# Stick-breaking attention inside a three-layer stack: running products of sigmoids in place of logarithms and suffix sums

## The reference, cut to what matters

```python
logits = einsum("bhtd,bhsd->bhts", q[:, :, s0:end], kb) * (Dh ** -0.5)
mask = s_idx[None, :] < t_idx[:, None]            # key strictly before query
log_keep = where(mask, log_sigmoid(-logits), 0.0)
after = sum(log_keep, -1, keepdims=True) - cumsum(log_keep, -1)
wts = where(mask, exp(log_sigmoid(logits) + after), 0.0)
outs.append(einsum("bhts,bhsd->bhtd", wts, vb))   # queries in blocks of 128
o = concatenate(outs) * silu(z)                   # z: a gate, 1024 channels
return o @ w_out
```

## Time and profile before

| | |
|---|---|
| median of three runs | 1218.24 us |
| the profiled execution: span from first to last instruction | 1214.8 us |
| what the runs' time has beside this span | 3.4 us |
| PE busy over the span | 96% |
| DVE, ACT, POOL busy over the span | 40%, 44%, 31% |
| stick-breaking stage, from the first piece of `last_gate` to the first `dense_unit` behind it | 628.1 to 753.4 us |

### The profile page before, as it was taken

How to read it: one execution, slowest core, us unless ns; L and a number is a source line. 1 busy time by engine, 2 the same in 40 slices (tenths; PEclk the granted TensorE clock), 3 DMA queues, 4 the chain that set the end, 5 groups by cost and what they waited for, 6 DMA issues and landing times.

```text
span 1214.8 us, 21306 instructions
## 1 busy us (share of the span) xinstructions
PE 1169.5 (96%) x8938; PEld 916.0 (75%) x8938; DVE 481.9 (40%) x903; ACT 539.0 (44%) x924; POOL 370.9 (31%) x148
## 2 busy tenths in 40 slices
PE   5999999989989999999999999999999999999898
PEld 3788886667668888777776667887887777678777
DVE  4575544553324382350314553640202333231563
ACT  4232246734336344542557774333135443753530
POOL 0133442233165414343431001323143231443161
PEclk7999999999999999999999999999999999999999
DMA  9723321386630232323423100333033411223301
GB/s 319 237 70 104 102 76 65 104 272 226 200 110 2 70 105 70 104 70 104 106 65 103 26 15 1 118 98 104 25 98 103 113 51 64 96 78 137 110 1 70
DMA packets 105761, 121.15 MB, mean 100 GB/s; under 512 B 5144, under 2 KB 91704, under 8 KB 105672
## 3 DMA queue, kind: packets, MB, share of 16 engines
q1 hardware_dynamic: 101424, 116.14, 30.2%
q10 hardware_dynamic: 4248, 3.73, 1.0%
HBM read 111.47 MB, written 2.10 MB: 93 GB/s over the span
## 4 chain that ended last, share of the span: by engine, by line
PE 84%; ACT 6%; DVE 4%; issue 3%; DMA 1%; ACTq 0%; SPq 0%; POOL 0%; DVEq 0%
PE ps L2043 41%; PE ps L2849 4%; PE ps L2663 3%; PE ps L2654 2%; PE ps L2089 2%; PE ps L2431 2%; PE ps L2184 2%; PE ps L2667 2%; PE ps L2693 2%; PE ps L2127 1%; PE ps L2207 1%; PE ps L2815 1%; PE ps L2260 1%; PE ps L2458 1%; PE ps L2802 1%
## 5 line engine op out<-in xcount | busy, mean ns | idle before, releaser
L606 POOL TENSOR_TENSOR wlo<-raw,whi 128x2048 fp32r<-128x2048 f32 x53 | 245.1, 4625 | 577.6 <-ACT whi L770 565.1
L770 ACT ACTIVATE whi<-raw 128x2048 fp32r<-128x2048 f32 x52 | 99.3, 1911 | 203.5 <-PE ps L2043 162.9
L612 POOL TENSOR_TENSOR wlo<-raw,whi 128x2048 fp32r<-128x2048 f32 x10 | 46.4, 4640 | 111.5 <-ACT whi L859 63.3
L1279 ACT ACTIVATE p<-sc,nmx 128x256 f32<-128x256 f32 x64 | 32.0, 501 | 47.0 <-PE ps L2802 45.8
L1870 DVE CUSTOM_DVE_ANT_0 sc<-ps,biast 128x256 f32<-128x256 f32 (+1 forms) x64 | 22.5, 393 | 66.8 <-PE ps L2791 37.9
L859 ACT ACTIVATE whi<-raw 128x2048 fp32r<-128x2048 f32 x11 | 21.1, 1917 | 62.8 <-PE ps L2043 62.8
L2043 PE MATMUL ps<-hC_hi,whi 128*128 128x512 f32 x184 | 47.1, 398 | 0.8 <-POOL wlo L606 0.8
L2043 PE MATMUL ps<-hC_lo,whi 128*128 128x512 f32 x184 | 45.6, 390 | 0.0
L2043 PE MATMUL ps<-hC_hi,wlo 128*128 128x512 f32 x184 | 45.4, 389 | 0.0
L2043 PEld LDWEIGHTS ps<-hC_hi,whi 128*128 128x128 f32 x184 | 33.8, 188 | 14.8 <-issue 6.4
L2043 PEld LDWEIGHTS ps<-hC_lo,whi 128*128 128x128 f32 x184 | 34.6, 188 | 7.4
(11 more groups left out here) (518 smaller groups left out, 2853.0 us busy)
## 6 DMA issues: line engine op xcount, KB each, us to landing
raw<-in_w_in_dram SPq DMA_DIRECT2D x24, 1024.0 KB, 5.2
raw<-in_w_in_a_dram SPq DMA_DIRECT2D x16, 1024.0 KB, 5.7
raw<-in_w_ada_dram SPq DMA_DIRECT2D x8, 1024.0 KB, 5.2
late_w<-in_w_ada_dram SPq DMA_DIRECT2D x8, 1024.0 KB, 6.1
raw<-in_w_kv_dram SPq DMA_DIRECT2D x8, 1024.0 KB, 5.1
raw<-in_w_in_b_dram SPq DMA_DIRECT2D x8, 1024.0 KB, 5.3
ada_a<-in_w_ada_dram SPq DMA_DIRECT2D x4, 1024.0 KB, 10.1
ada_b<-in_w_ada_dram SPq DMA_DIRECT2D x4, 1024.0 KB, 13.2
```

Source lines behind the costliest of these rows:

```text
L606: pool.tensor_tensor(wlo[:, s, :], raw[:, s, :], whi[:, s, :].bitcast(F32), ALU.subtract).then_inc(lo_ready, 1)
L612: pool.tensor_tensor(wlo[:, s, :], raw[:, s, :], whi[:, s, :].bitcast(F32), ALU.subtract).then_inc(lo_ready, 1)
L770: A(whi[:, s, :], raw[:, s, :], ACT.Copy).then_inc(hi_ready, 1)
L1279: A(p2[:, n % 2, 256 * e:256 * e + 256], sc2[:, n % 2, 256 * e:256 * e + 256], ACT.Exp, scale=-1.0, bias=nmx[:, grp, t, 2 * hp + e:2 * hp ...
```

## The change: what it does

Keys now lie along columns and queries along partitions; the product along the keys is a scan along a row. Two heads (one group kt) are worked together, in three rounds: the fourth block of queries (2 x 512 columns), the third (2 x 384), and the second with the first (2 x (256 + 128)). There are 24 rounds.

For round r: TensorE makes the scores of both heads at once, one on each half of the rows (`scores`); ACT makes sigmoid(-logit) (`keeps`) and sigmoid(logit) (`takes`) from PSUM; DVE turns the keeps into running products from the last key to the first, in place, by one scan instruction with a second operand `restart` that is 1 where the next head begins (`scans`, the third round has two scans); POOL multiplies takes by the products shifted by one key (`weights`); TensorE turns the weights by transposes (`turns`, three rounds later); ACT evacuates one head's half from PSUM and DVE the other's (`turned_first`, `turned_second`); TensorE multiplies with the values (`valued`, four rounds later). The swapped copies and SP's 32 transfers for them are gone. `yb_low` moves from DVE to POOL, and so do the last step of the last gate, now a sigmoid on ACT and a product on POOL, and all of the order around `first_out_b`. `kept` and `taken` have three buffers each.

```diff
+        ROUNDS = 3 * KD
+        TURNED, VALUED = 3, 4
+        def round_tiles(r):
+            return (((3, 0),), ((2, 0),), ((1, 0), (0, 256)))[r % 3]
+        def width(r):
+            return 384 if r % 3 else 512
+        def logits(r):
+            return ps[:, 2 * (r % 2):2 * (r % 2) + 2, 0:width(r)]
...
@@ POOL
-            for d in range(D_OUTB, len(blocks)):
+            split_lo(D_OUTB, 0)
+            def weights(r):
+                pool.wait_ge(scan_done, r + 1)
+                pool.wait_ge(taken_done, r + 1)
+                n = 2 * width(r)
+                pool.tensor_tensor(taken[:, r % 3, 0:n - 1], taken[:, r % 3, 0:n - 1], kept[:, r % 3, 1:n],
+                                   ALU.mult).then_inc(wts_done, 1)
...
+            for r in range(ROUNDS):
+                weights(r)
+                if r == 1:
+                    split_lo(D_OUTB, 1)
+                if r == 3:
+                    pool.wait_ge(last_silu, 1)
+                    pool.tensor_tensor(zsT[:, KD - 1, :], zsT[:, KD - 1, :], ybt[:, 1, :], ALU.mult).then_inc(last_silu, 1)
+                if r >= 8 and r % 3 == 2:
+                    yb_low((r - 8) // 3)
+            for kt in range(KD - 2, KD):
+                yb_low(kt)
+            for d in range(D_OUTB + 1, len(blocks)):
@@ ACT
+            def keeps(r):
+                act.wait_ge(scores_full, r + 1)
+                if r >= 3:
+                    act.wait_ge(wts_done, r - 2)
+                A(of_round(kept, r), logits(r), ACT.Sigmoid, scale=-1.0).then_inc(kept_done, 1)
+            def takes(r):
+                if r >= 3:
+                    act.wait_ge(turned_full, r - 2)
+                A(of_round(taken, r), logits(r), ACT.Sigmoid).then_inc(taken_done, 1)
...
+            for r in range(ROUNDS + TURNED):
+                if r < ROUNDS:
+                    keeps(r)
+                if r >= TURNED:
+                    turned_first(r - TURNED)
+                if r < ROUNDS:
+                    takes(r)
+                if r == 1:
                     next_hi(D_ZB + 1, 1)
...
@@ DVE
+            def scans(r):
+                dve.wait_ge(kept_done, r + 1)
...
+                n = width(r)
+                spans = ((0, 2 * n, 512 - n),) if r % 3 < 2 else ((0, n, 256), (n, 2 * n, 256))
+                for a, z, skip in spans:
+                    lo = max(a, 1)
+                    keep = kept[:, r % 3, z - 1:lo - 1:-1]
+                    last = dve.tensor_tensor_scan(keep, keep, restart[:, skip + z - a - 1:skip + lo - a - 1:-1]
+                                                  if skip + lo - a else restart[:, skip + z - a - 1::-1],
+                                                  1.0, ALU.mult, ALU.max)
+                last.then_inc(scan_done, 1)
...
+            for r in range(ROUNDS + TURNED):
+                if r >= TURNED:
+                    turned_second(r - TURNED)
+                if r < ROUNDS:
+                    scans(r)
...
+                if r >= 7 and r % 3 == 1:
+                    yb((r - 7) // 3)
@@ PE
+            def turns(r):
+                pe.wait_ge(wts_done, r + 1)
+                if r:
+                    pe.wait_ge(turned_act, r)
+                    pe.wait_ge(turned_dve, r)
+                for e in range(2):
+                    for b in range(width(r) // 128):
+                        at = width(r) * e + 128 * b
+                        last = pe.transpose(ps[:, 4 + e, 128 * b:128 * b + 128], taken[:, r % 3, at:at + 128], ident)
+                last.then_inc(turned_full, 1)
...
+            scores(0)
+            last_gate(range(12))
+            scores(1)
+            last_gate(range(12, 24))
+            for r in range(2, ROUNDS + VALUED):
+                if r < ROUNDS:
+                    scores(r)
+                if r == ROUNDS + 1:
+                    first_out_b(range(2))
+                if r == ROUNDS + 3:
+                    first_out_b(range(2, KD - 1))
+                if TURNED <= r < ROUNDS + TURNED:
+                    turns(r - TURNED)
+                if r >= VALUED:
+                    valued(r - VALUED)
+            first_out_b(range(KD - 1, KD))
```

More of the change, by code:

```diff
@@ L14 @@
 LN_EXP = "natural_log_exp_and_others"
+SIGMOID = "sigmoid_and_others"
 T, D = 512, 1024
@@ L2632, in last_gate, with scores @@
                         last.then_inc(dense_full, 1)
-            last_gate(range(8))
             pe.wait_ge(kqn_done, 16)
             pe.wait_ge(bf_ready, 1)
-            def qk(n):
-                s, kt = n % 2, n // 2
-                rs, other = slice(64 * s, 64 * s + 64), slice(64 - 64 * s, 128 - 64 * s)
-                if n == 0:
+            def scores(r):
+                kt = r // 3
+                if r == 0:
                     pe.wait_ge(gate_done, 7)
-                pe.wait_ge(swapped[kt % 2], 64 * (kt // 2 + 1))
-                for j in range(NT):
-                    if n >= 2 and j < 2:
-                        pe.wait_ge(wt_done, 2 * (n - 2) + 1 + j)
-                    if j:
-                        at = 128 * j - 128
-                        k, q = swk[other, kt % 2, at:at + 128], swq[other, kt % 2, at:384]
-                    else:
-                        k, q = kTb[rs, kt, 0:128], qTb[rs, kt, :]
-                    mm(logits(n, j), k, q, start=j != 3, stop=True, skip_group_check=True)
-                for j in range(NT):
-                    last = mm(logits(n, j)[:, 0:128], bandbf[:, 0, :], bandbf[:, 1, :], start=False, stop=True,
-                              skip_group_check=True)
-                last.then_inc(qk_full, 1)
@@ L2696, in weighted @@
-                if blocks[-1] == 2:
-                    last.then_inc(pv_full, 1)
+                for i, at in round_tiles(r):
+                    for j in range(i + 1):
+                        for e in range(2):
+                            n = 2 * kt + e
+                            last = mm(ps[side(e), 6 + kt % 2, 128 * i:128 * i + 128], Vb[:, j, 64 * n:64 * n + 64],
+                                      turned(r)[:, width(r) * e + at + 128 * j:width(r) * e + at + 128 * j + 128],
+                                      start=j == 0, stop=j == i, skip_group_check=True)
@@ L2699, in first_out_b @@
+                last.then_inc(pv_full, 1)
             def first_out_b(ks):
```

214 lines of the change are left out of this document (60 added, 154 removed).

## The result

The changed kernel took 1209.7 us (median of four runs, 1207.6 to 1211.1) where the kernel before took 1218.0 on the same chip: ratio 0.9931, interval 0.9914 to 0.9949, so it is 0.7% faster. A second set of four runs gave 1209.35 and 0.9923 (0.9898 to 0.9948). The forecast was 1218.6, no change. The traced execution has a span of 1208.1 us and lasted 1210.0.

The account below looks back on a forecast made before the run. The prediction took DVE's scans and POOL's work as one line: last product at 738.6 us, stage end 752.9 against 753.4, clock loss 0.9, so span +0.4 on 1214.8, plus 3.4: 1218.6 us, range 1198 to 1232.

Parts of the forecast that it names:

- The bound: In the changed stage, DVE's scans and POOL's work exclude each other and form one line, 12.98 us per group against 13.18.
- The scan's unit: DVE's scan at the slow end, 2.11 ns a column: 2.16 us for 1023 columns, 1.62 for 767; 39.4 in rounds 2 to 23.
- POOL's product: POOL's product of weights in each round: 2.39 us for 1023 columns, 1.83 for 767; 44.2 in rounds 2 to 23.
- 0.08 for POOL to start: POOL starts 0.08 us behind each of three scans per group; 22 starts add 1.8 us in rounds 2 to 23.
- Start: Stage start: rounds 0 and 1, the last gate and its copy; the second product ends at 640.9 us.
- Tail: After the last product at 738.6: TensorE work 9.8 us, uncovered steps 3.1, six products 1.4; 0.9 added for lost clock.
- the 3.4 us beside the span: Time the runs have beside the profiled span of 1214.8 us, added to reach the forecast time.
- Rival 1: DVE's scan runs at the plain pass's rate: 1202 us, or some 1188 if POOL did not hold scans; chance 0.17.
- Rival 2: TensorE's granted clock falls through the stage, under 0.58 in the mean, making TensorE the bound: 1234 us; chance 0.16.
- The wide range: Whole forecast range of 1198 to 1232 us, taking in the slow and plain scan cases and most of the fallen-clock case.
- the likeliest case's own range: 1213 to 1226 us: starts of 0 to 0.3 us at some 44 changes, half the clock's loss, one or two stalls.
- the forecast case: The stage set by the line of scans and POOL's work: 1218.6 us, chance 0.67; inside it 0.25 faster, 0.35 slower.

Follow-up runs that it names:

- `psum`: Changed kernel with the scan's restart row in PSUM, one bank for value sums, scans split per head, gate product ahead of the older weights' copy: 1194.18 us.
- `best`: Changed kernel with restart row in PSUM, POOL's weight block after the last product, last value sums before projection products, gate product between two scans: 1179.26 us.
- `aligned`: Changed kernel with POOL's product reading its second operand without the one-column offset: 1215.73 us, ratio 0.9964 to the kernel before.
- `val_first`: Changed kernel with TensorE issuing the last round's value sums ahead of the 30 projection products: 1203.86 us, ratio 0.9884 to the kernel before.

## Why the prediction was wrong, point by point

- **The bound: right.** DVE's scans and POOL's work form one line; TensorE's 40 us of gain is spent on it. `psum` gives back 15 us of it, and `best`, with start and tail mended too, nearly all.
- **The scan's unit: right end, small miss.** 2.29 and 1.75 for 2.16 and 1.62, 2.11 ns for each further column. Over rounds 2 to 23, seven at 2.29, seven at 1.75 and eight at 0.94 + 0.93 (the lengths of `psum`) are 43.2, not 39.4: 3.8 us too little. The Trainium skill, "DVE: opcode table, instruction layouts, handler registers and perf-mode slots" (Datapath and trigger behaviour), says that the built-in scan runs at half throughput. The trace agrees: 2.11 ns a column against 1.04 for a plain pass over two operands ((2.28 - 0.68) / 1536).
- **POOL's product: mis-sized.** "2.39 for 1023 and 1.83 for 767" was read off rows whose operands begin alike; this product reads its second operand one column on and takes 2.00 and 1.54. The sum is 37.1 and not 44.2: 7.1 too much. `aligned` puts that price back, and its line is 6.8 us longer, its median 6.0.
- **The step that failed most: "0.08 for POOL to start", "22 starts 1.8", and in the range "starts of 0 to 0.3 us at each of some 44 changes".** The cost is below zero. With the lengths alone the line is 43.2 + 37.1 + 4.5 + 1.3 + 6.4 = 92.5 us; measured from 641.04 (639.50 + 1.54) to 726.81 (725.27 + 1.54) it is 85.8. That is 6.7 less over some 44 changes, 0.15 each, where I had added 1.8: 8.5 too much. A product starts 0.08 behind its scan only where it had not been issued before; in a steady group that is one of three (725.27, above). I had sign and size in my hands: a held DVE pass "ended 0.55 after POOL, under its own 0.68", 0.13 less, and POOL's held product of 2.61 us ended 1.15 after DVE's pass, under its own 1.29, 0.14 less. I used the first for "costs nothing" and didn't let it become a gain. Why a held instruction is cheaper, no run tells.
- The three make 3.8 - 7.1 - 8.5 = -11.8; the low parts at 1.27 are 0.1 less; 97.7 became 85.8. That the result missed by less than that is luck: the scans and the tail were priced too low.
- **Start: right, in part by errors that cancel.** 640.9 forecast, 641.04 measured, the block of weights in the line behind it, as said. The copy of the last gate ended 0.4 later and the scan took 0.1 longer than forecast, and the product was 0.3 shorter.
- **Tail: 18.7 us, not 14.3 + 0.9.** The first twelve projection products were to be done before the last product, but POOL's late weights kept TensorE until 722.28, and 1.9 us of them and 1.2 of transposes and values came behind 726.81; 1.5 of this is the clock that had fallen at 722 to 726 and that `val_first`'s execution kept. The gap was 2.8 (3.1 forecast); the clock behind it cost 1.5 here and 0.4 in the second trace, and not 0.9.
- So the stage ended at 745.52, not at 753.8: 8.3 of the 8.9 us. The traced span gave 1.2 back in later stages, and the 3.4 us beside the span were 1.9. In every run with both figures the time lies about 2 us over the span of its own cores, so the 3.4 will have set a median beside the span of a shorter execution.
- **Rival 1** has the wrong mechanism: the scan isn't fast, and it is held. That its 1202 lay nearer the result than my 1218.6 (7.7 us off against 8.9) is an accident. **Rival 2** is refuted: the granted clock was 1.00 from 654 to 722 with TensorE busy for 54 of 68 us and about a quarter of its products transposes (123 of 519). Transposes alone no run here shows.

The wide range held the time, the likeliest case's own range (1213 to 1226) did not. The two large errors had one sign, and I had given the forecast case 0.35 slower to 0.25 faster on the ground that overlooked waits only add.

## What to carry to other kernels

Ask of each pair on DVE and POOL how many operands lie in SBUF; one operand in PSUM took them apart and was worth 15 us in `psum`. Price an instruction in such a line by what it adds behind the other's end, and not by its length alone plus a start; where the profile before shows a held instruction, its row holds that figure. Take a price from a row whose operands begin as the new ones do.

## What the runs showed of the hardware that I had not expected

- POOL's two-operand pass over float32 is faster when the second operand starts one or two columns into its tile, the first at the start of its own: 1.09 against 1.27 us for 511 columns, 2.00 against 2.36 for 1023. Why, no run tells.
- Two engines that exclude each other hand over at a gain: 0.14 to 0.20 us less for a held instruction than for a free one, and 11.20 us for a group whose instructions take 12.26 alone.
- The granted clock scatters by execution: two executions of the changed kernel had 0.91 and 1.00 in the stretch 1160 to 1180, far behind the change.
